# Value product of the latent attention turned round: values stationary, probabilities streamed, softmax sums on VectorE

## What is computed

```python
q_all = (rms_norm(a_cq, cq_norm[l]) @ w_uq[l]).reshape(B, S, A_HEADS, A_DQK)   # 128 + 64 rotary
kv = (rms_norm(a_ckv, ckv_norm[l]) @ w_ukv[l]).reshape(B, S, A_HEADS, A_NOPE + A_DV)
# per 128-query block, causal:
s = jnp.einsum('bhqd,bshd->bhqs', qi, k).astype(jnp.float32) * scale
s = jnp.where(k_pos[None, :] <= q_pos[:, None], s, -jnp.inf)
p = jax.nn.softmax(s, axis=-1)
o = jnp.einsum('bhqs,bshd->bqhd', p.astype(v.dtype), v)
ha = o * jax.nn.silu(a_z)          # a_z = 1024 columns of h @ w_in
merged = g_m * (hm @ w_br_m[l]) + g_a * (ha @ w_br_a[l]) + g_c * (hc @ w_br_c[l])
```

## Time and profile before

| | us |
|---|---|
| median of 3 runs | 2946.66 (2935.18 to 2951.58) |
| the profiled execution | 2922.08 |
| span of its slowest core (core 5) | 2921.0 |
| spans of all cores | 2886.8 to 2921.0 |
| TensorE busy | 2707.9 (93%) |
| VectorE busy | 937.9 (32%) |
| ScalarE busy | 772.3 (26%) |
| GpSimd busy | 399.7 (14%) |

### The profile page before, as it was taken

How to read it: one execution, slowest core, us unless ns; L and a number is a source line. 1 busy time by engine, 2 the same in 40 slices (tenths; PEclk the granted TensorE clock), 3 DMA queues, 4 the chain that set the end, 5 groups by cost and what they waited for, 6 DMA issues and landing times.

```text
span 2921.0 us, 42383 instructions; the slowest of 8 cores (2886.8 to 2921.0 us)
## 1 busy us (share of the span) xinstructions
PE 2707.9 (93%) x14237; PEld 1305.9 (45%) x14237; DVE 937.9 (32%) x1778; ACT 772.3 (26%) x1551; POOL 399.7 (14%) x566
## 2 busy tenths in 40 slices
PE   5999998988899999799999989999997899999997
PEld 2545443433444444355555544444443444444443
DVE  3455763354544433233322242111121211111123
ACT  4322322112333353244444342111111111111111
POOL 1000000131122121000000000332210122122110
PEclk9999999999999999899999999999998999999999
DMA  9647453053453655526424477557546644444343
GB/s 258 167 87 166 97 103 72 19 112 96 96 112 67 156 142 121 125 60 132 124 65 98 104 193 197 128 114 138 120 88 215 205 76 76 78 75 77 65 116 144
DMA packets 186580, 342.02 MB, mean 117 GB/s; under 512 B 46272, under 2 KB 140800, under 8 KB 176128
## 3 DMA queue, kind: packets, MB, share of 16 engines
q0 software_dynamic: 20160, 138.26, 27.8%
q1 hardware_dynamic: 166208, 201.05, 23.5%
HBM read 391.23 MB, written 86.28 MB: 163 GB/s over the span
## 4 chain that ended last, share of the span: by engine, by line
PE 80%; DMA 11%; DVE 4%; issue 2%; ACT 2%; SPq 1%; POOL 1%; DVEq 0%; ACTq 0%; POOLq 0%
PE bk L1401 21%; PE bk L460 20%; PE bk L449 13%; PE bk L1409 10%; PE bk L1559 5%; PE bk L1239 2%; PE bk L1210 2%; PE bk L1212 2%; DMA out<-m_xo 2%; DMA m_wgb<-wGB 1%; DMA ACC<-m_tmpc 1%; DMA MG<-m_t 1%; DMA m_bif<-bif 1%; DMA m_mv<-MV 1%; DMA m_cq<-CQT 1%
## 5 line engine op out<-in xcount | busy, mean ns | idle before, releaser
L460 PE MATMUL bk<-m_w,m_hT 128*128 128x512 bf16 x3072 | 731.2, 384 | 14.1 <-DVE m_t L740 10.0
L1401 PE MATMUL bk<-m_hT,m_wgb 128*128 128x512 bf16 x3072 | 708.5, 380 | 3.4 <-DMA m_wgb<-wGB 3.4
L1401 PEld LDWEIGHTS bk<-m_hT,m_wgb 128*128 128x128 bf16 x3072 | 299.0, 98 | 355.2 <-issue 7.7
L460 PEld LDWEIGHTS bk<-m_w,m_hT 128*128 128x128 bf16 x3072 | 299.8, 99 | 349.1 <-issue 31.4
L1409 PE MATMUL bk<-m_hb,m_wgb 128*128 128x512 bf16 x1536 | 369.4, 381 | 12.7 <-DMA m_hb<-HMT 7.5
L449 PE MATMUL bk<-m_hT,m_w 128*128 128x512 bf16 (+1 forms) x1600 | 366.9, 382 | 14.0 <-ACT m_t L791 7.2
L1414 DVE SCALAR_TENSOR_TENSOR m_tmpc<-m_sg,bk 128x512 f32<-128x512 f32 x160 | 109.8, 688 | 653.3 <-PE bk L1401 423.3
L1406 ACT ACTIVATE m_sg<-bk 128x512 f32<-128x512 f32 x192 | 114.8, 598 | 768.7 <-PE bk L1401 714.2
L449 PEld LDWEIGHTS bk<-m_hT,m_w 128*128 128x128 bf16 (+1 forms) x1600 | 156.7, 99 | 200.4 <-issue 27.6
L1409 PEld LDWEIGHTS bk<-m_hb,m_wgb 128*128 128x128 bf16 x1536 | 150.0, 98 | 192.1 <-issue 17.4
L1215 ACT ACTIVATE m_Pa<-bk 128x512 bf16<-128x512 f32 (+1 forms) x320 | 168.8, 534 | 248.3 <-PE bk L1212 149.3
(11 more groups left out here) (179 smaller groups left out, 2173.9 us busy)
## 6 DMA issues: line engine op xcount, KB each, us to landing
m_wgb<-wGB POOLq DMA_DIRECT2D x96, 768.0 KB, 7.7
m_w<-wA POOLq DMA_DIRECT2D x16, 2048.0 KB, 19.7
m_xt<-x SPq DMA_DIRECT2D x16, 1024.0 KB, 12.9
m_xo<-x SPq DMA_DIRECT2D x16, 1024.0 KB, 5.6
out<-m_xo SPq DMA_DIRECT2D x15, 1024.0 KB, 5.8
m_w<-wMEM POOLq DMA_DIRECT2D x4, 2048.0 KB, 16.8
ACC<-m_tmpc SPq DMA_DIRECT2D x32, 256.0 KB, 7.0
m_accl<-ACC SPq DMA_DIRECT2D x16, 512.0 KB, 7.0
```

Of the source, the lines that this page charges most:

```text
L460: fw.op("pe", lambda e: e.matmul(bk[:, 0:ncols], lhsT=src(kc, tt * 128, 128), rhs=w[:, kc, 0:ncols], start=(kc == 0), stop=(kc == KC - 1)) ...
L1401: fw.op("pe", lambda e: e.matmul(gb[:, 0:512], lhsT=w[:, kc, :], rhs=h0[:, kc, tcs], start=(kc == 0), stop=(kc == 15)), reads=[w.r] + h0.r ...
```

## The change

- The value product is turned round: `vx[:, kt, :]` (128x128) is stationary, `P` streams, up to 512 columns, one matmul for each item (320), result with features on partitions, in one bank. Two banks (2, 3) take turns block by block; scores get four banks (4 to 7), are made three items ahead instead of two, and are issued before the item's value product; six `P` tiles instead of four.
- The softmax sums leave TensorE's stream: VectorE adds each `P` into a float32 tile `acc`. At the block's end `closing()` splits `acc` into two bf16 tiles (ScalarE copy, VectorE difference), sums over the partitions with two 512-column matmuls against a tile of 2.0, copies one row to SBUF, stores it to `DEN` in memory, loads it back as 32x16, takes the reciprocal on VectorE, stores that to `REC`, loads it as a broadcast to 128 partitions, and multiplies on GpSimd. The steps are spread over the following items: for a block whose last item is L the row sums are issued after item L+3, the load of `DEN` after L+6, the reciprocal after L+9, the broadcast load after L+10, the multiplication after L+11.
- At the block's end VectorE multiplies the bank by the gate tile into `u` (two tiles). No transposes, no `tail`.
- The gate is made with features on partitions (`az_block`, `unit_fm`), `AZ` is [1024, S], loaded for each block as 128 rows of 1 KB. `mla` waits for a head's gate only at that head. Four of twelve `t16` tiles are freed before.
- `HAT` is stored for each block. `light` yields 3.61 instead of 3.53 for each count of `mlstm`, with the total adjusted.

```diff
-    AZ_d = dscr("AZ", [S, 1024])
+    AZ_d = dscr("AZ", [1024, S])
...
-    m_AZ = [Multi(16) for _ in range(2)]
+    m_AZ = [Multi(4) for _ in range(8)]
...
-    m_HA = [Multi(8) for _ in range(2)]
+    m_HA = [Multi(16) for _ in range(2)]
...
+    DEN_d = dscr("DEN", [32, 512], F32)
+    REC_d = dscr("REC", [32, 512], F32)
+    m_DEN = [Multi() for _ in range(32)]
+    m_REC = [Multi() for _ in range(32)]
...
-        all_az0 = []
+        az_heads = []
+
+        def az_block(blk, bank):
+            w = wq.use(I_AZ[blk])
+            for ci in range(4):
+                h = blk * 4 + ci
+                for tb in range(4):
+                    def ev(ps, r_ps):
+                        t32, t16 = nxt_t32(), nxt_t16()
+                        fw.op("act", lambda e: e.activation(out=t32[:], in_=ps, func=AF.Tanh, scale=0.5), reads=[r_ps], writes=[t32.r])
+                        fw.op("dve", lambda e: e.scalar_tensor_tensor(out=t16[:], in0=t32[:], scalar=1.0, in1=ps, op0=ALU.add, op1=ALU.mult),
+                              reads=[t32.r, r_ps], writes=[t16.r])
+                        fw.store(AZ_d[h * 128:(h + 1) * 128, tb * 512:(tb + 1) * 512], t16[:], reads=[t16.r], to=m_AZ[h])
+                    yield from unit_fm(w, ci * 128, 128, hsrc, hres, 16, tb, bank(), ev)
+                az_heads.append(h)
+            wq.done(I_AZ[blk])
...
-            yield from gate_block(I_AZ[0], AZ_d, 0, m_AZ[0], d2_banks)
-            all_az0.append(True)
+            ar.free(t16s[8:])
+            del t16s[8:]
+            yield from az_block(0, d2_banks)
...
-            vxs, _ = mk("vx", 2, [128, 16, 132], BF16)
-            azs, _ = mk("az", 2, [128, 16, 128], BF16)
-            haTs, nxt_haT = mk("haT", 2, [128, 1024], BF16)
-            Ps, nxt_P = mk("Pa", 4, [128, 512], BF16)
-            hat, nxt_hat = mk("hat", 8, [128, 128], BF16)
-            stB, nxt_st = mk("stB", 4, [128, 8], F32)
+            vxs, _ = mk("vx", 2, [128, 16, 128], BF16)
+            azs, nxt_az = mk("az", 2, [128, 512], BF16)
+            Ps, nxt_P = mk("Pa", 6, [128, 512], BF16)
+            sums, nxt_sum = mk("sumP", 2, [128, 512], F32)
+            his, nxt_hi = mk("hi", 1, [128, 512], BF16)
+            los, nxt_lo = mk("lo", 1, [128, 512], BF16)
+            us, nxt_u = mk("u", 2, [128, 512], F32)
+            recs, nxt_rec = mk("rec", 2, [128, 512], F32)
+            dns, nxt_dn = mk("dn", 2, [32, 32], F32)
+            haTs, nxt_haT = mk("haT", 1, [128, 512], BF16)
+            twos = ar.alloc("twos", [128, 128], BF16)
+            fw.op("dve", lambda e: e.memset(twos[:], 2.0), writes=[twos.r])
...
-            for vx in vxs:
-                fw.op("dve", lambda e: e.memset(vx[:, :, 128:129], 2.0), writes=[vx.r])
...
+            o_banks, q_banks = bankset(2, 3), bankset(4, 5, 6, 7)
...
-            def load_az(h):
-                s = h % 2
-                fw.dma("sp", azs[s][:], AZ_d[:, h * 128:(h + 1) * 128].rearrange("(t p) c -> p t c", p=128),
-                       reads=[m_AZ[h // 4]], writes=[azs[s].r])
...
+            AHEAD = 3
...
-                bs, r_bs = s_banks()
+                bs, r_bs = q_banks()
...
+            def closing(h, qb, acc, u):
+                k = 4 * h + qb
+                hi, lo = nxt_hi(), nxt_lo()
+                fw.op("act", lambda e: e.copy(out=hi[:], in_=acc[:]), reads=[acc.r], writes=[hi.r])
+                fw.op("dve", lambda e: e.tensor_tensor(out=lo[:], in0=acc[:], in1=hi[:], op=ALU.subtract), reads=[acc.r, hi.r], writes=[lo.r])
+                yield 3
+                bd, r_bd = q_banks()
+                for part in (hi, lo):
+                    fw.op("pe", lambda e: e.matmul(bd[:, 0:512], lhsT=twos[:], rhs=part[:], start=(part is hi), stop=(part is lo)),
+                          reads=[twos.r, part.r], writes=[r_bd])
+                rec = nxt_rec()
+                fw.op("act", lambda e: e.copy(out=rec[0:1, :], in_=bd[0:1, 0:512]), reads=[r_bd], writes=[rec.r])
+                fw.store(DEN_d[k:k + 1, :], rec[0:1, :], reads=[rec.r], to=m_DEN[k])
+                yield 3
+                dn = nxt_dn()
+                fw.dma("sp", dn[:, 0:16], DEN_d[k:k + 1, :].rearrange("o (p c) -> (o p) c", c=16), reads=[m_DEN[k]], writes=[dn.r])
+                yield 3
+                fw.op("dve", lambda e: e.reciprocal(out=dn[:, 16:32], in_=dn[:, 0:16]), reads=[dn.r], writes=[dn.r])
+                fw.store(REC_d[k:k + 1, :].rearrange("o (p c) -> (o p) c", c=16), dn[:, 16:32], reads=[dn.r], to=m_REC[k])
+                yield 1
+                fw.dma("sp", rec[:], REC_d[k:k + 1, :].partition_broadcast(128), reads=[m_REC[k]], writes=[rec.r])
+                yield 1
+                haT = nxt_haT()
+                fw.op("pool", lambda e: e.tensor_tensor(out=haT[:], in0=u[:], in1=rec[:], op=ALU.mult), reads=[u.r, rec.r], writes=[haT.r])
+                fw.store(HAT_d[h * 128:(h + 1) * 128, qb * 512:(qb + 1) * 512], haT[:], reads=[haT.r], to=m_HA[qb // 2])
+                yield 0
+
+            ends = []
+
+            def step(e):
+                c = next(e[1], None)
+                if c is None:
+                    ends.remove(e)
+                else:
+                    e[0] = c
+
+            def advance():
+                for e in list(ends):
+                    e[0] -= 1
+                    if e[0] <= 0:
+                        step(e)
 
...
-            while not all_az0:
-                yield 1
-            for n in range(2):
+            for n in range(AHEAD):
                 scores(n)
                 yield 1
             for n, (h, qb, kt) in enumerate(items):
-                vx, az = vxs[h % 2], azs[h % 2]
-                P, q_lo = wait_P.pop(n)
-                for qt in range(q_lo, 4 * qb + 4):
-                    jj = qt - q_lo
-                    bo, r_bo = o_of(qt - 4 * qb)
-                    fw.op("pe", lambda e: e.matmul(bo, lhsT=P[:, jj * 128:(jj + 1) * 128], rhs=vx[:, kt, 0:129],
-                                                   start=(kt == 0), stop=(kt == qt)),
-                          reads=[P.r, vx.r], writes=[r_bo])
-                if n == 1:
-                    load_az(0)
+                vx = vxs[h % 2]
+                last = 4 * qb + 3
+                if kt == 0:
+                    while h not in az_heads:
+                        yield 1
+                    az = nxt_az()
+                    fw.dma("sp", az[:], AZ_d[h * 128:(h + 1) * 128, qb * 512:(qb + 1) * 512], reads=[m_AZ[h]], writes=[az.r])
+                    bo, r_bo = o_banks()
+                    acc = nxt_sum()
+                P = live_P[n]
+                q_lo = max(kt, 4 * qb)
+                off = (q_lo - 4 * qb) * 128
+                ncols = 512 - off
+                if n + AHEAD < len(items):
+                    scores(n + AHEAD)
+                fw.op("pe", lambda e: e.matmul(bo[:, off:512], lhsT=vx[:, kt, :], rhs=P[:, 0:ncols], start=(kt == 0), stop=(kt == last)),
+                      reads=[P.r, vx.r], writes=[r_bo])
+                if qb == 0 and kt == 0:
+                    fw.op("dve", lambda e: e.tensor_copy(out=acc[:], in_=P[:]), reads=[P.r], writes=[acc.r])
+                elif kt == 1 and qb > 0:
+                    P0 = live_P[n - 1]
+                    fw.op("dve", lambda e: e.tensor_tensor(out=acc[:], in0=P0[:], in1=P[:], op=ALU.add), reads=[P0.r, P.r], writes=[acc.r])
+                elif kt > 0:
+                    fw.op("dve", lambda e: e.tensor_tensor(out=acc[:, off:512], in0=acc[:, off:512], in1=P[:, 0:ncols], op=ALU.add),
+                          reads=[P.r, acc.r], writes=[acc.r])
+                live_P.pop(n - 1, None)
                 if qb == 1 and kt == 0 and h + 1 < 8:
-                    load_az(h + 1)
-                if n + 2 < len(items):
-                    scores(n + 2)
-                if kt == 2 and tails:
-                    tails.pop(0)()
-                if kt < 4 * qb + 3:
+                advance()
+                yield 1
+                if kt == last:
+                    while len(ends) > 1:
+                        step(ends[0])
+                    u = nxt_u()
+                    fw.op("dve", lambda e: e.tensor_tensor(out=u[:], in0=bo[:, 0:512], in1=az[:], op=ALU.mult), reads=[r_bo, az.r], writes=[u.r])
+                    e = [0, closing(h, qb, acc, u)]
+                    ends.append(e)
+                    step(e)
                     yield 1
-                    continue
-                has = []
-                for q4 in range(4):
-                    qt = 4 * qb + q4
-                    bo, r_bo = o_of(q4)
-                    sc = nxt_st()
-                    fw.op("dve", lambda e: e.reciprocal(out=sc[:, 0:1], in_=bo[:, 128:129]), reads=[r_bo], writes=[sc.r])
-                    ha = nxt_hat()
-                    fw.op("dve", lambda e: e.scalar_tensor_tensor(out=ha[:], in0=bo[:, 0:128], scalar=sc[:, 0:1], in1=az[:, qt, :],
```

(23 more changed lines are left out.)

18 lines of the change are left out of this document (4 added, 14 removed).

## The result

The changed kernel is slower: 2991.99 us for its profiled execution, where the forecast had 2920 for that execution and the kernel before took 2922.08. Its other comparable execution took 3002.35. The ratio to the kernel before on the same chip is 1.0212, 95% interval 1.0142 to 1.0282; by it the median of 2946.66 becomes 3009. The forecast of 2945, its likeliest case "no change" and the whole range up to 2982 are wrong; the rival "the chain becomes the bound in bursts" (2990 at its worst) named VectorE's stands as the way, with 0.25, though not the reader that passes them on.

A forecast was written before the change was run, and what follows sets the result against it. TensorE, busy 93% of the span, was taken as the bound; -35.7 us of waits, +5.9 of its own work and +28 of chain stalls gave -2: 2920 us profiled, 2945 median, likeliest range 2932 to 2961, wider 2912 to 2982.

The forecast's parts named there:

- the chain becomes the bound in bursts: Rival: VectorE standing over 6 items at the reciprocal or u holds masks and tiles; 2990, middle case 2967; chance 0.25.
- The waits that go: TensorE's waits in mla, 32.3 us, and 3.4 us at half clock disappear: -35.7 us, between -20 and -36.
- TensorE's own work: In mla: value products -0.9 us, transposes removed -7.0, row sums added +13.8; net +5.9 us.
- The turning round: Swapping the value product's operands gains nothing itself, weight loads being hidden; a rival gain to 2918 had chance 0.02.
- VectorE is no bound: VectorE's busy share in mla rises from 28 to about 62 in 100 without becoming the bound; taken at 0.
- how long VectorE may stand: In the closing chain: VectorE may stand about 6 items, 7.7 us, or 3 items, 3.8 us, where masks are behind it.
- Beside a head's loads: DEN's load queues behind the next head's loads, delaying reciprocal and product: 1 us for each of 7 heads, +7 (0 to 28).
- the quiet chain: Closing's trip through memory away from bursts: 5.0 us before the reciprocal, 6.3 after; mostly hidden, 0 to 1 us in all.
- The terms for the bursts: Chain stalls beside the 2048 KB fetch in head 1, +6 us, and the first wGB fetches in head 3, +11.
- The single fetches: Chain stalls beside single 768 KB fetches, every 20 us at the end: +4 us (0 to 8).
- The term left out: the clock: After TensorE stands: 3.4 us of half clock removed with the old waits; 3 us per new stand only in a rival.
- Shifted collisions: Transfers meeting at other places after the changed mix of light and mlstm: 0, with ±4 us.

The follow-up runs named there:

- e1: Changed kernel without the trip through memory: ScalarE copies the sums to SBUF, GpSimd multiplies by them uninverted; 0.9868 of the kernel before, 2878 and 2879 us.
- e10: Changed kernel with the inversion kept on chip, no memory trip, only the bf16 sum tile summed; 0.9891 of the kernel before, 2896 us profiled.
- e14: Changed kernel, memory trip kept, with three tiles of u, rec and dn and a closing of 22 items instead of 11; 0.9897 of the kernel before.
- e12b: Changed kernel with the reciprocals moved from VectorE to GpSimd as a power of -1; 1.0373 of the kernel before.
- e4: Changed kernel with row sums six items after a block's end instead of three, one tile each of hi and lo (layer no longer computed); 1.0258.
- e4b: Changed kernel with row sums six items after a block's end instead of three, two tiles each of hi and lo; 2988 and 3012 us.
- e5: Changed kernel with three tiles of u and rec instead of two, four t16 tiles fewer; 1.0151 of the kernel before.
- e9: Changed kernel with the load of DEN, store and load of REC and store of HAT on GpSimd's queue instead of SP's; 1.0197 of the kernel before.

## Why the prediction failed

**Right.** The waits that go, and that little else moves: without any chain stall the terms give -35.7 + 5.9 = -30 us. The mean span fell by 43 in e1, which has the changed kernel's work on TensorE, by 28 in e10 and by 16 in e14, each with the stand of some 8 us at the first value product in it. The +5.9 of TensorE's own work is below what these traces resolve (2674 before, 2668 after). The turning round brings nothing by itself; a full item, changed kernel, beside the earlier trace rows:

```profile
1313.24 0.38 PE L1231 MATMUL bk<-m_qn,m_kn 128*128 128x512 bf16 x1
1313.45 0.38 PE L1233 MATMUL bk<-m_qr,m_kr 128*128 128x512 bf16 x1
1313.67 0.38 PE L1306 MATMUL bk<-m_Pa,m_vx 128*128 128x512 bf16 x1
1313.88 1.03 PE L464 MATMUL bk<-m_w,m_hT 128*128 128x512 bf16 x4
```

0.21 us for one matmul of 512 columns where four of 129 took 0.22. VectorE is no bound: 332 of 540 us busy in e14 (core 0), 61 in 100 for 62 forecast (luck in part: the prediction's own terms, 133 + 45 + 44 - 45 - 34 = 143 us in the 475 of `mla`, are 30 in 100 more and give 58). The chain in a quiet place: reciprocal at 1243.59 (core 0, block 2 of head 0), product done at 1250.28, 6.7 us for 6.3; `REC` was sized too long here (issue to the broadcast's issue 1.4 for 2.4) and the broadcast too short (3.5 for 2.6), so the sum fits by luck; in head 7 `REC` took 3.3 with next to nothing in flight.

**The step that failed: how long VectorE may stand.** The prediction put it at six items, 7.7 us, from the `P` tiles, and three for a few masks. It named the two row-sum matmuls as work and not as a reader. They come three items after a block's end and need `lo`, which is behind `u` in VectorE's queue, and a stand at the reciprocal just before has used most of that: some 0.4 us was left in head 1. By that bound every wait at `u` or at the reciprocal next to a block's end reaches TensorE: the limit in block 1 was L+15, where the prediction had L+18 or L+19. "Beside a head's loads" was 1 us for each of 7 heads; the waits were 24.7 us on core 0 and 24 to 36 on the others. Six of the seven stand beside a head's loads (21.7 us on core 0), since head 7 loads none; the seventh, 3.05 us there, belongs to the quiet chain, which was put at 0 to 1 us in all. That `haT` comes late and holds `u` was in the text. An obvious remedy wasn't tried: `lo` ahead of `u` in VectorE's queue.

**The terms for the bursts** were about right. The 2048 KB fetch and the first `wGB` burst stood with 6 and 11 us; the two longest stands at L1251 are theirs, 8.1 and 7.5 us on core 0, 17 together in the mean over the cores. The way of the first was foreseen as well, `REC` and then `az` behind it. Timeline of core 0, from the store that was issued 1.9 us after a 2048 KB fetch at 1299.09:

```profile
1300.99 0.30 SPq L140 DMA_DIRECT2D REC<-m_dn  x1
1315.66 0.34 SPq L140 DMA_DIRECT2D m_rec<-REC  x1
1320.42 0.34 SPq L140 DMA_DIRECT2D HAT<-m_haT  x1
...
1322.37 0.34 SPq L140 DMA_DIRECT2D m_az<-AZ  x1
```

```profile
1323.87 0.69 DVE L1325 TENSOR_TENSOR m_u<-bk,m_az 128x512 f32<-128x512 f32 x1 [11.31 <-DMA m_az<-AZ]
...
1325.31 0.58 PE L1251 MATMUL bk<-m_lo,m_twos 128*128 128x512 bf16 x1 [8.13 <-DVE m_Pa L1238]
```

SP stands 14.3 us for `REC`, then for GpSimd's product to store `HAT`, and only then issues `az`, which VectorE needs. A 2 KB store beside a 2 MB fetch, 14.3 us late, stopped VectorE and TensorE too. Behind the `wGB` burst issued at 1427.31 the same happens with the `REC` of 1440.69, and VectorE stands 11.08 us. The single fetches stood with 4: the waits that ended at 1652.31 (5.9 us, for `lo`) and at 1687.77 (4.7, for `hi`) follow fetches of 1641.11 and 1666.57, behind which `az` and `REC` came 8.7 and 7.6 us after their issue. So of the forecast's 28 us of chain stalls, against 52.6 on core 0, the missing part is the head loads (7 for 21.7), the quiet chain (0 to 1 for 3.1) and the single fetches (4 for 10.6).

**The term left out: the clock.** The sum took 3.4 us of half clock off and wrote "3 us each" only into a rival. Measured over the cores it is +29 us while TensorE is busy. After the stand that ended at 1464.15, core 0 (length, busy PE, PEld, DVE, ACT, POOL, PEclk):

```profile
1465.00:1472.00 7.00, 7.00 (x27) 2.97 (x26) 2.78 (x6) 2.62 (x6) 0.00 (x0) 0.66 1.00 237
```

27 matmuls in 7 us, where 0.215 each would give 32; the 0.66 is half clock at first and 0.81 from 1468 on. For cores 0 and 1 also ran at 0.81 for long, 148 us each between 1333 and 1495, which is some 7 of the 29 us. The rows are 1400 to 1430 of core 1 and of core 3:

```profile
1400.00:1430.00 30.00, 30.00 (x124) 13.08 (x123) 17.65 (x35) 14.20 (x27) 3.39 (x5) 0.81 0.83 201
...
1400.00:1430.00 30.00, 26.93 (x131) 12.47 (x130) 17.07 (x35) 14.19 (x27) 5.16 (x6) 0.99 0.59 122
```

In the kernel before all eight cores have 1.00 there. Core 1 was never idle and did 124 matmuls where core 3, idle for 3 us, did 131. Why two cores of a die fell to 0.81 wasn't tried. It came once more, on cores 6 and 7 of e12b (136 and 130 us), and in none of e1, e4, e4b, e5, e9, e10 and e14. The Trainium skill ("TensorE: Matmul & The Clock Gate", Part 1) names 13/16 of the clock as a third state, which it gives for a whole die at once; the value agrees with these 0.81, the extent doesn't, since core 3 of the same die had 0.99.

**Shifted collisions** were "0, with ±4". The fetch moved from 1194.63 (core 5 before) to 1181.52 (core 0 after) and met the values' load, 8 us; and the first load of `cq` after `mla` is waited for 10.8 us on core 0, where core 5 of the kernel before had 3.0 at most. That `cq` wait stays in e14, 7.6 to 15.1 us on seven cores and 4.8 on one, and is at most 4.4 in e1, e9 and e10: it comes with the trip on the SP queue, by what way stays open.

**In sum**, over the cores: forecast -2, of it +2 for waits and work and -3 for the clock; measured +62, of it +33 and +29. The room that the readers had is the cause of both, as e14 shows: with the room widened, idle time goes from 240 to 188 us and the clock lost while busy from 59 to 34. Only why the 0.81 came is open.

## What to carry to other kernels

Before a chain through memory is put into an in-order queue, list every reader of everything queued behind each of its waits, the new instructions included, and take the smallest slack, in microseconds at the place where the items are short. Then give the chain tiles and items for its worst landing, all at once: e4b and e5 each loosened one link and moved the stand to the next, and of the variants that keep the trip only e14 paid. Price a stand of TensorE with what the clock does after it, counted over TensorE's busy time alone; here that was 29 us on top of 39 more of idle time.
